# Down-projection units in another order, the final root made per token and transposed, and the squares of a norm in one running sum

## The chip, the cores and the metric

The kernel runs on one core of a Trainium2 chip. The metric is the device time of one execution in microseconds (us), as the median of several runs. The engines are named as in the profile: PE (matrix products), DVE (VectorE), ACT (ScalarE), POOL (GpSimd) and SP (which issues DMAs here).

## The reference

Three transformer layers on 256 tokens of width 1024, in float32. Layer A is a pooling layer, layer B a stick-breaking attention layer, and both end in a gated feed-forward part; a final norm follows, and a second block with attention, a recurrence and a gated output. What the change touches, cut to the core:

```python
def rmsnorm(x, g):
    return x * lax.rsqrt(jnp.mean(x * x, axis=-1, keepdims=True) + EPS) * g

def swiglu(h, w_gu, w_down):                      # D_FF = 2816 = 22 tiles of 128
    gate, up = jnp.split(h @ w_gu, 2, axis=-1)
    return (jax.nn.silu(gate) * up) @ w_down

x = x + swiglu(rmsnorm(x, norm_ffn), w_gu, w_down)      # layers A and B
...
y = merged @ w_out                                # second block, its last part
h = h + _rms_norm(y, g_post)
e = p @ w_ple_up
h = h + jax.nn.sigmoid(h @ w_ple_gate) * e
```

## The kernel before

Activations lie transposed in SBUF: channels on the 128 partitions (8 tiles, `X[:, m, :]`), the 256 tokens along the free dimension. Every float32 operand of the large products is split in an upper part (a copy rounded to fp32r on ACT: `hi`, `XH`, `HH`) and a lower part (the difference, on DVE: `lo`, `XL`, `HL`), and a product is three matmuls, upper by upper, upper by lower and lower by upper (`product`, lines 573 to 575), or two where upper and lower part of the activations stand beside each other (`wide_product`, lines 579 and 580: 256 and 512 columns).

Weights come in units of 1 MB (or 704 KB for a down unit) through four slots. SP loads unit u as soon as PE has finished unit u - 4 (`unit_done`); ACT and DVE split a unit two units ahead of PE, in halves. The order of the work on every engine is a list written out by hand (`plan`), which each engine runs through with its own handlers; engines meet by counting semaphores.

**The feed-forward part.** `gu` computes 22 units, one for each tile of H: PE, then ACT and DVE take the sum, scale it by the norm's root, apply silu, and write `HH` and `HL` (lines 1598 to 1615 and 2259 to 2275). `evac_done` counts the units taken out of PSUM. `down` then computes 8 tiles of the residual from 16 units of 11 tiles each: unit 2m is the first half (h = 0, tiles 0 to 10 of H) of tile m, and unit 2m + 1 the second (h = 1, tiles 11 to 21). The units of even and odd tiles go to two banks of PSUM (`DOWN[turn]`). PE waits for 11 tiles of H ahead of the first unit, and for all 22 ahead of each unit with h = 1. All 16 units run in a loop of four steps. After the second half of a tile DVE adds the two halves of the bank to X (lines 2309 and 2311), ACT writes XH and DVE XL, and POOL squares the tile.

**The norms.** There are eight (n = 0 to 7). POOL squares the 8 tiles and adds them up in two running sums, the even tiles in `ACC[:, 0, :]` and the odd ones in `ACC[:, 1, :]` (`squares`, from line 2916). PE multiplies both by a matrix of ones (lines 664 and 665), so that every partition holds the sum for every token in `STAT`; these are float32 matmuls, which run as two passes each. Where a column per token is wanted as well (n = 3), four more products with one column follow (line 674). DVE scales (line 2089) and takes the reciprocal (2090), ACT the square root (1521).

**The last norm** (n = 7) is that of `y`, between the output projection (`unit_out2`) and the gate (`unit_egate`). DVE copies each pair of tiles of y out of PSUM to `SGT[:, 8:16, :]` (line 2813), ACT squares that copy (1990), and POOL adds up six of the eight squares; PE takes the last two itself (line 669). DVE makes a reciprocal of 256 columns, ACT its root, and `post` on DVE multiplies each tile of y by weight and root and adds it to X (2833, 2835), ACT and DVE split it (1517, 2081), and PE begins the gate with tile 0 (`pair_of`). Between them PE has four short up projections `eup(0)` to `eup(3)` (12 matmuls each, taken out by ACT at line 2001), and eight filler matmuls with ones (`keep_busy`, line 975), which wait for the reciprocal. ACT and DVE split the weights of the second gate unit in that stretch (lines 1773 and 2492), DVE the second half between tiles 0 and 1 of `post`.

```python
second += [("eup", 0), ("stats", 7, 0), ("eup", 1), ("root",), ("eup", 2), ("eup", 3), ("post",)]
```

## Time and profile before

| | us |
|---|---|
| median of 3 runs | 891.33 |
| lowest and highest | 889.78, 893.73 |
| the profiled execution | 892.28 |
| its span, first to last instruction | 890.2 |
| PE busy in it | 872.7 |
| DVE busy | 671.9 |
| ACT busy | 483.4 |
| POOL busy | 115.3 |

Busy time of PE counts each matmul with its whole latency, and these overlap, so that the busy time lies closer to the span than the work of PE does. A start in a timeline is therefore read against the next start. The profiled execution is one execution, 0.95 us above the median.

### The profile page before, as it was taken

How to read it: one execution, taken by the hardware profiler on the slowest of the kernel's cores; microseconds unless marked ns; L12 is line 12 of the kernel's file. 1: busy time of each engine (PE TensorE's matmuls, PEld its weight loads, DVE VectorE, ACT ScalarE, POOL GpSimd, SP SyncE). 2: the span in 40 equal slices, each digit the busy share in tenths (PEclk: the TensorE clock that was granted, in tenths of full speed). 3: DMA queues.
4: the chain of work that ended last, by engine and by line, in shares of the span. 5: the costliest groups of instructions: out<-in, count | busy, mean ns of one | idle time of the engine just before them, and what ended most of it. 6: DMA issues, size and time to landing. Idle time of an engine off the chain costs nothing. (4 is left out here: it accounts for less than half of the span.)

```text
span 890.2 us, 19346 instructions
## 1 busy us (share of the span) xinstructions
PE 872.7 (98%) x7632; PEld 793.1 (89%) x7632; DVE 671.9 (75%) x999; ACT 483.4 (54%) x779; POOL 115.3 (13%) x133
## 2 busy tenths in 40 slices
PE   7999999999999999999999999999999999999998
PEld 7998888888889988898888888899999888899998
DVE  6996887777677776868777767786996777747785
ACT  5674465555545566745555554458624554534453
POOL 2002300000022000050000006640008010000000
PEclk8999999999999999999999999999999999999999
DMA  9443455554557432254555445674534343244441
GB/s 339 176 162 121 154 184 188 186 186 144 171 190 250 149 136 98 93 190 160 182 183 184 175 151 184 203 261 159 180 131 132 122 130 79 95 141 143 167 166 48
DMA packets 23409, 144.48 MB, mean 162 GB/s; under 512 B 2968, under 2 KB 3224, under 8 KB 9648
## 3 DMA queue, kind: packets, MB, share of 16 engines
q1 hardware_dynamic: 22032, 140.26, 45.5%
q0 software_dynamic: 1168, 3.23, 1.6%
q8 instruction: 49, 0.80, 0.4%
q14 instruction: 16, 0.13, 0.0%
q10 hardware_dynamic: 144, 0.06, 0.0%
HBM read 142.47 MB, written 1.06 MB: 161 GB/s over the span
## 5 line engine op out<-in xcount | busy, mean ns | idle before, releaser
L2067 DVE TENSOR_TENSOR lo<-raw,hi 128x1024 fp32r<-128x1024 f32 (+1 forms) x210 | 243.9, 1203 | 12.2 <-ACT hi L1483 8.6
L580 PE MATMUL ps<-X,hi 128*128 128x512 f32 x704 | 249.0, 398 | 0.0
L579 PE MATMUL ps<-X,lo 128*128 128x256 f32 x704 | 198.4, 282 | 0.6 <-DVE X L2082 0.6
L573 PE MATMUL ps<-X,hi 128*128 128x256 f32 x600 | 174.1, 290 | 0.8 <-DVE X L2081 0.7
L574 PE MATMUL ps<-X,hi 128*128 128x256 f32 x600 | 169.7, 283 | 0.0
L575 PE MATMUL ps<-X,lo 128*128 128x256 f32 x600 | 169.6, 283 | 0.0
L580 PEld LDWEIGHTS ps<-X,hi 128*128 128x128 f32 x704 | 132.3, 188 | 32.7
L579 PEld LDWEIGHTS ps<-X,lo 128*128 128x128 f32 x704 | 133.0, 189 | 1.8 <-issue 1.2
L580 PE MATMUL ps<-H,hi 128*128 128x512 f32 x352 | 122.4, 392 | 0.0
L1483 ACT ACTIVATE hi<-raw 128x1024 fp32r<-128x1024 f32 (+1 forms) x109 | 107.7, 988 | 25.0 <-DMA raw<-in_down 13.6
L573 PEld LDWEIGHTS ps<-X,hi 128*128 128x128 f32 x600 | 114.8, 191 | 5.4 <-issue 3.9
L574 PEld LDWEIGHTS ps<-X,hi 128*128 128x128 f32 x600 | 115.0, 192 | 0.4 <-issue 0.2
L575 PEld LDWEIGHTS ps<-X,lo 128*128 128x128 f32 x600 | 114.9, 192 | 0.0
L2492 DVE TENSOR_TENSOR lo<-raw,hi 128x1024 fp32r<-128x1024 f32 x68 | 84.0, 1236 | 30.3 <-ACT hi L1773 23.7
L1486 ACT ACTIVATE hi<-raw 128x1024 fp32r<-128x1024 f32 (+1 forms) x109 | 103.7, 951 | 0.2 <-DMA raw<-in_wide 0.2
L579 PE MATMUL ps<-H,lo 128*128 128x256 f32 x352 | 98.7, 280 | 2.6 <-DVE H L2275 2.6
L580 PEld LDWEIGHTS ps<-H,hi 128*128 128x128 f32 x352 | 65.8, 187 | 14.5
L579 PEld LDWEIGHTS ps<-H,lo 128*128 128x128 f32 x352 | 66.5, 189 | 3.2 <-issue 3.2
L573 PE MATMUL ps<-H,hi 128*128 128x256 f32 x224 | 65.9, 294 | 2.9 <-DVE H L2082 2.6
L574 PE MATMUL ps<-H,hi 128*128 128x256 f32 x224 | 64.5, 288 | 0.0
L575 PE MATMUL ps<-H,lo 128*128 128x256 f32 x224 | 64.5, 288 | 0.0
L1615 ACT ACTIVATE H<-GU 128x256 f32 (+1 forms) x44 | 18.4, 418 | 82.4 <-DVE GU L2268 82.4
(394 smaller groups left out, 1448.7 us busy)
## 6 DMA issues: line engine op xcount, KB each, us to landing
raw<-in_wide SPq DMA_DIRECT2D x106, 1024.0 KB, 4.9
raw<-in_down SPq DMA_DIRECT2D x32, 704.0 KB, 4.1
BI<-bias_table POOLq DMA_DIRECT2D x16, 128.0 KB, 4.8
raw<-in_wide SPq DMA_DIRECT2D x3, 512.0 KB, 9.0
X<-in_x SPq DMA_DIRECT2D x1, 1024.0 KB, 13.0
WG<-in_group SPq DMA_DIRECT2D x1, 768.0 KB, 17.1
out<-X SPq DMA_DIRECT2D x3, 256.0 KB, 2.4
cmask<-in_masks POOLq DMA_DIRECT2D x1, 544.0 KB, 5.9
```

Source lines behind the costliest of these rows:

```text
L573: nc.tensor.matmul(dst, wh, xh, start=first, stop=False, skip_group_check=True)
L574: nc.tensor.matmul(dst, wh, xl, start=False, stop=False, skip_group_check=True)
L575: return nc.tensor.matmul(dst, wl, xh, start=False, stop=last, skip_group_check=True)
L579: nc.tensor.matmul(bank[:, 0:T], wl, x[:, 0, :], start=first, stop=False, skip_group_check=True)
L580: return nc.tensor.matmul(bank, wh, x, start=False, stop=last, skip_group_check=True)
L1483: nc.scalar.activation(hi[:, s, 0:h], raw[:, s, 0:h], ACT.Copy).then_inc(hi_ready, 1)
L1486: nc.scalar.activation(hi[:, s, h:n], raw[:, s, h:n], ACT.Copy).then_inc(hi_ready, 1)
L1615: nc.scalar.activation(dst, src, ACT.Copy).then_inc(hh_ready, 1)
L2067: nc.vector.tensor_tensor(lo[:, s, a:b], raw[:, s, a:b], hi[:, s, a:b].bitcast(F32), ALU.subtract).then_inc(lo_ready, 1)
L2492: nc.vector.tensor_tensor(lo[:, u % 4, part], raw[:, u % 4, part], hi[:, u % 4, part].bitcast(F32), ALU.subtract).then_inc(lo_ready, 1)
```

## The change

The diff has three parts. (1) `down` computes its first four units in the order tile 0 first half, tile 1 first half, tile 0 second half, tile 1 second half, unrolled ahead of the loop, which has a pass less; the weights in HBM lie in that order. (2) The squares of a norm go in one running sum, and PE multiplies that one by ones. (3) The last norm's sum is one column per token; scaling, reciprocal and root are made on that column ([128 x 2]), and PE transposes the root, broadcast along the free dimension, to `STAT`, where `post` reads it. ACT squares the last pair of y from PSUM, DVE copies it after that, the weight splits of the second gate unit stand elsewhere in the lists of ACT and DVE, and the filler matmuls are left out.

```diff
+DN_FIRST = [(0, 0), (1, 0), (0, 1), (1, 1)]
+DN_REST = [(m, h) for m in range(2, KD) for h in range(2)]
...
 # PE, stats(n)
-                pe.wait_ge(sq_done, 8 * (n - 1) if n < 6 else 8 * (n - 2) - 2)
-                nc.tensor.matmul(STAT[:, 0:T], ones[:, :], ACC[:, 0, :], start=True, stop=False, skip_group_check=True)
-                last = nc.tensor.matmul(STAT[:, 0:T], ones[:, :], ACC[:, 1, :], start=False, stop=True, skip_group_check=True)
                 if n == 7:
-                    pe.wait_ge(y_sq, 4)
-                    for m in (6, 7):
-                        last = nc.tensor.matmul(STAT[:, 0:T], ones[:, :], SGT[:, m, :], start=False, stop=(m == 7),
-                                                skip_group_check=True)
+                    pe.wait_ge(sq_done, 8 * (n - 2) - 2)
+                    for q, tile in enumerate((ACC[:, 0, :], SGT[:, 6, :], SGT[:, 7, :])):
+                        if q == 1:
+                            pe.wait_ge(y_sq, 4)
+                        for i in range(2):
+                            last = nc.tensor.matmul(STAT[:, T + i:T + i + 1], tile[:, i * P:(i + 1) * P], ones[:, 0:1],
+                                                    start=(q == 0 and i == 0), stop=(q == 2), skip_group_check=True)
+                    last.then_inc(stat_done, 1)
+                    return
+                pe.wait_ge(sq_done, 8 * (n - 1))
+                last = nc.tensor.matmul(STAT[:, 0:T], ones[:, :], ACC[:, 0, :], start=True, stop=True, skip_group_check=True)
                 if cols:
                     for i in range(2):
-                        for b in range(2):
-                            last = nc.tensor.matmul(STAT[:, T + i:T + i + 1], ACC[:, b, i * P:(i + 1) * P], ones[:, 0:1],
-                                                    start=False, stop=(b == 1), skip_group_check=True)
+                        last = nc.tensor.matmul(STAT[:, T + i:T + i + 1], ACC[:, 0, i * P:(i + 1) * P], ones[:, 0:1],
+                                                start=False, stop=True, skip_group_check=True)
...
 # PE, down(u0): half(u, s, turn, h)
                     if h == 0:
+                        if half_i[0] is None:
+                            bank_free(g0 + turn)
                         else:
+                            pe.wait_ge(evac_done, half_i[0] * 2 + (g0 + turn + 1))
                     if h == 1:
                         pe.wait_ge(hl_ready, N_GU * (layer + 1))
...
-                with pe.Fori(0, N_DN // 4) as i:
+                for j, (m, h) in enumerate(DN_FIRST):
+                    half(u0 + j, (u0 + j) % 4, m, h)
+                with pe.Fori(0, N_DN // 4 - 1) as i:
                     half_i[0] = i
                     for j in range(4):
-                        half(i * 4 + (u0 + j), (u0 + j) % 4)
+                        half(i * 4 + (u0 + 4 + j), (u0 + j) % 4, j // 2, j % 2)
...
 # PE
+            def root():
+                pe.wait_ge(rs_done, 8)
+                for i in range(2):
+                    last = nc.tensor.transpose(STAT[:, i * P:(i + 1) * P], RSC[:, 1, i:i + 1].to_broadcast([P, P]), ident[:, :])
+                last.then_inc(root_in, 1)
...
                 if u == U_EGATE:
-                    pe.wait_ge(rv_done, 8)
-                    keep_busy(8)
...
 # ACT, down: the same four units ahead of its loop; unit_out2(u)
+                if j == 2:
+                    ahead(u + 1)
                 act.wait_ge(xl_ready, 48)
+                if j < 3:
+                    act.wait_ge(evac_done, first_group(u) + 1)
+                    src = SGT[:, 8 + 2 * j:10 + 2 * j, :]
+                else:
+                    act.wait_ge(unit_done, u + 1)
+                    src = PROJ[first_group(u) % 2][:, :].rearrange("p (a b) -> p a b", a=2)
+                nc.scalar.activation(SGT[:, 2 * j:2 * j + 2, :], src, ACT.Square).then_inc(y_sq, 1)
+                if j == 1:
                     ahead(u + 1)
+                if j == 3:
+                    split_half(U_EGATE + 1, 0)
...
 # ACT, eup(j)
-                if j < 2:
-                    split_half(U_EGATE + 1, j)
+                if j == 0:
+                    split_half(U_EGATE + 1, 1)
+
+            def root_column():                       # at ("stats", 7, 0)
+                act.wait_ge(rv_done, 8)
+                nc.scalar.activation(RSC[:, 1, :], RV[:, T:T + 2], ACT.Sqrt).then_inc(rs_done, 1)
...
 # DVE, down: the same four units ahead of its loop; unit_out2(u)
                 dve.wait_ge(unit_done, u + 1)
+                if j == 3:
+                    dve.wait_ge(y_sq, 4)
                 nc.vector.tensor_copy(SGT[:, 8 + 2 * j:10 + 2 * j, :], halves(bank_of(u))).then_inc(evac_done, 1)
...
+                if j == 3:
+                    split_half(U_EGATE + 1, 0)
+
+            def root_column():                       # at ("stats", 7, 0)
+                dve.wait_ge(stat_done, 8)
+                need(dve, rs_done, 7)
+                link(nc.vector.tensor_scalar(RV[:, T:T + 2], STAT[:, T:T + 2], 1.0 / D, EPS, ALU.mult, ALU.add))
+                nc.vector.reciprocal(RV[:, T:T + 2], RV[:, T:T + 2]).then_inc(rv_done, 1)
+                split_half(U_EGATE + 1, 1)
...
 # DVE, post()
-                dve.wait_ge(rs_done, 8)
+                dve.wait_ge(root_in, 1)
...
-                    link(nc.vector.scalar_tensor_tensor(SGT[:, 8 + m, :], SGT[:, 8 + m, :], vec[:, c:c + 1], RS[:, 1, :],
+                    link(nc.vector.scalar_tensor_tensor(SGT[:, 8 + m, :], SGT[:, 8 + m, :], vec[:, c:c + 1], STAT[:, 0:T],
...
-                    if m == 0:
-                        split_half(U_EGATE + 1, 1)
-                    else:
+                    if m > 0:
                         lower_of(m - 1)
...
 # POOL, squares(n, m, src)
-                if m < 2:
-                    nc.gpsimd.tensor_tensor(ACC[:, h, :], src, src, ALU.mult).then_inc(sq_done, 1)
+                if m == 0:
+                    nc.gpsimd.tensor_tensor(ACC[:, 0, :], src, src, ALU.mult).then_inc(sq_done, 1)
                 else:
                     link(nc.gpsimd.tensor_tensor(SQT[:, h, :], src, src, ALU.mult))
                     pool.wait_ge(sq_done, 8 * n + m)
-                    nc.gpsimd.tensor_tensor(ACC[:, h, :], ACC[:, h, :], SQT[:, h, :], ALU.add).then_inc(sq_done, 1)
+                    nc.gpsimd.tensor_tensor(ACC[:, 0, :], ACC[:, 0, :], SQT[:, h, :], ALU.add).then_inc(sq_done, 1)
```

## Rows read from the trace of the kernel before

**Rows 1.** The page: busy time of each engine; granted clock in 40 slices.

```profile
PE 872.7 (98%) x7632; PEld 793.1 (89%) x7632; DVE 671.9 (75%) x999; ACT 483.4 (54%) x779; POOL 115.3 (13%) x133
...
PEclk8999999999999999999999999999999999999999
```

**Rows 2.** Waits of PE: line, releaser, us in total, times, longest us.

```profile
PE ps L579 <- DVE H L2275: 2.6, 2, 1.3
```

**Rows 3.** Timeline of PE, both down projections: start us, us, what [idle].

```profile
225.04 0.28 PE L579 MATMUL ps<-H,lo 128*128 128x256 f32 x1
...
225.39 0.28 PE L579 MATMUL ps<-H,lo 128*128 128x256 f32 x1
...
227.20 0.36 PE L579 MATMUL ps<-H,lo 128*128 128x256 f32 x1 [1.30 <-DVE H L2275]
...
527.06 0.36 PE L579 MATMUL ps<-H,lo 128*128 128x256 f32 x1 [1.30 <-DVE H L2275]
```

**Rows 4.** Timeline of DVE, last gate-up unit of the first layer.

```profile
222.69 0.69 DVE L2259 TENSOR_TENSOR GU<-GU,ps 128x512 f32<-128x512 f32 x1 [1.39 <-ACT GU L1598]
...
226.52 0.43 DVE L2275 TENSOR_TENSOR H<-GU,H 128x256 fp32r<-128x256 f32 x1 [0.48 <-ACT H L1615]
```

**Rows 5.** Timeline of PE, sums of the third and fourth norm.

```profile
102.28 0.59 PE L664 MATMUL ps<-ACC,ones 128*128 128x256 f32 x2
102.71 0.59 PE L665 MATMUL ps<-ACC,ones 128*128 128x256 f32 x2
...
291.09 0.95 PE L674 MATMUL ps<-ones,ACC 128*128 128x1 f32 x8
```

**Rows 6.** Timeline of PE, sum of the last norm to the first gate unit.

```profile
853.86 0.59 PE L664 MATMUL ps<-ACC,ones 128*128 128x256 f32 x2
...
855.78 0.47 PE L573 MATMUL ps<-PH,hi 128*128 128x256 f32 x1
...
860.21 1.95 PE L975 MATMUL ps<-ones 128*128 128x128 f32 x16
862.89 0.36 PE L573 MATMUL ps<-X,hi 128*128 128x256 f32 x1 [0.73 <-DVE X L2081]
```

**Rows 7.** Timeline of DVE, same stretch.

```profile
856.17 0.42 DVE L2089 TENSOR_SCALAR RV<-ps 128x256 f32<-128x256 f32 x1 [1.89 <-PE ps L669]
856.63 1.75 DVE L2090 RECIPROCAL RV<-RV 128x256 f32<-128x256 f32 x1
...
859.47 0.48 DVE L2833 SCALAR_TENSOR_TENSOR SGT<-SGT,vec,RS 128x256 f32<-128x256 f32 x1
...
860.33 1.22 DVE L2492 TENSOR_TENSOR lo<-raw,hi 128x1024 fp32r<-128x1024 f32 x1
...
862.32 0.42 DVE L2081 TENSOR_TENSOR X<-X 128x256 fp32r<-128x256 f32 x1
```

**Rows 8.** Timeline of ACT, same stretch.

```profile
854.32 0.63 ACT L1990 ACTIVATE SGT<-SGT 128x512 f32<-128x512 f32 x1 [2.66 <-DVE SGT L2813]
...
858.08 1.05 ACT L1773 ACTIVATE hi<-raw 128x1024 fp32r<-128x1024 f32 x1
...
859.34 0.59 ACT L2001 ACTIVATE E<-ps 128x512 f32<-128x512 f32 x1
```

**Rows 9.** Single lines (ns min/median/max), and four transposes in the timeline.

```profile
L2309 DVE TENSOR_TENSOR X<-X,ps x16: 420/422/422, 231.4 to 584.5; 128x256 f32 x12, 128x256 f32<-128x256 f32 x4
...
L2642 DVE TENSOR_SCALAR NM<-MX x8: 169/170/171, 692.7 to 754.3; 128x2 f32<-128x2 f32 x8
...
L1523 ACT ACTIVATE RSC<-RV x3: 187/187/188, 24.3 to 595.0; 128x2 f32<-128x2 f32 x3
...
700.47 0.60 PE L1141 MATMUL ps<-ident,PR 128*128 128x128 f32 x4
```

**Rows 10.** Windows, PE: stretch, us, busy (matmuls), clock, DMA share, GB/s.

```profile
9.00:15.00 6.00, 5.02 (x23) 0.52 1.02 398
16.00:20.00 4.00, 4.00 (x36) 1.00 1.01 424
```

More of the change, by code:

```diff
@@ L1630, in half @@
                         split_hi(u + AHEAD, (s + AHEAD) % 4, n)
-                    if (s - u0) % 2 == 1:
+                    if m is not None:
                         act.wait_ge(x_done, m + (8 + 16 * layer + 1))
@@ L2300, in tile, with half @@
                     return a[:, bass.ds(m, 1)] if a is gains else a[:, bass.ds(m, 1), :]
-                def half(u, s, n, m):
-                    odd = (s - u0) % 2 == 1
-                    turn = ((s - u0) % 4) // 2
-                    count = m + (8 + 16 * layer + 1)
+                def half(u, s, n, m, turn):
+                    odd = m is not None
                     if odd:
+                        count = m + (8 + 16 * layer + 1)
                         dve.wait_ge(unit_done, u + 1)
@@ L2322, in half @@
                         split_lo(u + AHEAD, (s + AHEAD) % 4, n)
-                with dve.Fori(0, N_DN // 4 - 1) as i:
+                for j, (m, h) in enumerate(DN_FIRST):
+                    half(u0 + j, (u0 + j) % 4, DN_TILES * P, m if h else None, m)
+                with dve.Fori(0, N_DN // 4 - 2) as i:
                     for j in range(4):
-                        half(i * 4 + (u0 + j), (u0 + j) % 4, DN_TILES * P, i * 2 + j // 2)
+                        half(i * 4 + (u0 + 4 + j), (u0 + j) % 4, DN_TILES * P, i * 2 + (2 + j // 2) if j % 2 else None, j // 2)
                 for j in range(N_DN - 4, N_DN):
                     u = u0 + j
-                    half(u, u % 4, width(u + AHEAD) if u + AHEAD < N_UNITS else 0, j // 2)
+                    half(u, u % 4, width(u + AHEAD) if u + AHEAD < N_UNITS else 0, j // 2 if j % 2 else None, (j % 4) // 2)
             def unit_k(u):
@@ L3038, in down_units @@
 def down_units(w):
-    t = tiles(w).transpose(1, 0, 2, 3)
-    return t.reshape(N_DN, DN_TILES, P, P).transpose(0, 2, 1, 3).reshape(-1, P, DN_TILES * P)
+    t = tiles(w).transpose(1, 0, 2, 3).reshape(KD, 2, DN_TILES, P, P)
+    t = np.stack([t[m, h] for m, h in DN_FIRST + DN_REST])
+    return t.transpose(0, 2, 1, 3).reshape(-1, P, DN_TILES * P)
 def columns(v):
```

33 lines of the change are left out of this document (13 added, 20 removed).

## The prediction

> **What bounds the kernel now.** The page comes first: PE is busy for 872.7 of 890.2 us and its granted clock is full in all slices but the first [rows 1]. So work of PE in the middle of the kernel costs its own time, and what the other engines do costs only where PE waits for them. The next view is PE's list of waits. Its largest entry that the change touches is two waits of 1.3 us, together 2.6 us, for H [rows 2]. The timeline of PE around them is third: they stand at the start of the two down projections. In the dense stretch one 256-column matmul of line 579 follows another after 0.35 us (225.04 to 225.39), but the next starts at 227.20, which is 1.81 us later, so PE loses 1.46 us there, and the same idle time of 1.30 us stands at 527.06 [rows 3]. The page says busy for a matmul's whole latency, so the idle time is shorter than the loss. Last come the timelines of PE, DVE and ACT from 853.86 us, where the last norm's root is made: PE fills part of the wait with eight filler matmuls (1.95 us) and is then idle for 0.73 us more before the gate's first matmul at 862.89 [rows 6].
>
> The profiled execution took 892.28 us, 2.1 us more than its span. The median of the three runs is 891.33, so 0.95 us are taken off when the sum goes over to the median.
>
> **Down units in another order.** The work is the same: as many matmuls, copies, splits and loads, of the same sizes. What moves is the second unit. Before, unit 2 of each layer is the upper half of tile 0, which needs all 22 tiles of H; the last of them is ready at 226.95 (526.9 in the second layer), when line 2275 ends [rows 4]. After, unit 2 is the lower half of tile 1, which needs the first 11 tiles only. PE reaches it at about 225.75. It does wait for one thing more, the evacuation of the last gate-up unit, because the bank check asks for the count of that unit; line 2259 did that at 222.69 and is done at 223.38 [rows 4], 2.4 us early. A down unit takes 11 times 0.35 = 3.9 us [rows 3], so the first unit that needs all of H comes at 225.75 + 3.9 = 229.6, 2.7 us after it is ready. The stall goes, and nothing is late next: 1.46 us for each layer, **2.9 us** in all. Tiles 0 and 1 are now finished one unit apart instead of two, so DVE has two sets of residual additions and lower splits in consecutive units, and POOL two tiles of squares. DVE's additions and lower split go in a unit's 3.9 us at 75% mean load [rows 1] and it had two units without additions before that, so I count nothing. If this cover is not there, the unit after waits and the ends of this term are 0 and 2.9 us.
>
> **One running sum of squares.** Four norms (the third, fourth, fifth and the last) add up their squares in one tile instead of two. In three of them PE drops one product with the matrix of ones. It goes as two passes, and the pair takes 102.71 - 102.28 = 0.43 us [rows 5], with PE dense before and after it, so 3 x 0.43 = 1.3 us. The fourth norm also has eight passes of one column, 0.95 us [rows 5], and half of them go: 0.45 us. Together **1.7 us**. POOL gets one addition more for each norm, at tile 1; it is busy for 13% of the span [rows 1] and the sum is asked for a unit later, so that is hidden. Without that cover the added addition (1 to 1.5 us of POOL) would be PE's wait in three places and this term would be -2.5 us at worst; since the last tile's work on POOL is unchanged, I see no way to it.
>
> **The final root.** The old chain, by the timelines: the sum's products run from 853.86 to 855.78 and include a wait for the square of the last two tiles; DVE starts at 856.17 with 256 columns, and its reciprocal takes 1.75 us; a half weight split lies before the first tile of the residual (859.47) and another of 1.22 us between that tile and the next (860.33), so that the first lower tile starts at 862.32 and PE at 862.89 [rows 6, 7].
>
> The new chain, step by step. ScalarE squares the last tiles straight from PSUM, so it no longer waits for the copy on DVE, and the square (0.63 us [rows 8]) is done before PE asks for it at 853.86. PE then has twelve passes of one column; eight took 0.95 us [rows 5], so 1.4 us, to 855.3 instead of 855.78. Three units of the small up projection took 860.21 - 855.78 = 4.43 us, 1.48 each [rows 6]: the first of them ends at 856.75. In its shadow DVE scales and inverts a [128 x 2] column: the scaling costs 0.17 us [rows 9] and I take as much for the reciprocal of two columns, where 256 took 1.75. With the 0.39 us from the products' end to DVE's start (855.78 to 856.17) and 0.1 us of signals that is 856.1; the root on ACT takes 0.19 us [rows 9], 856.4. PE therefore finds it ready, makes two transposes (four took 0.60 us [rows 9], so 0.3) and is at 857.05, and after two more units at **860.0**. That is PE's own side.
>
> The other side: DVE sees the transposed root at 857.45; the first tile takes 0.86 us (859.47 to 860.33 [rows 7]) and is there at 858.3. ACT is late next: by its order it copies the third up unit, done at about 858.7, first, 0.59 us [rows 8], and splits the residual's tile after it, 0.42 us, so at 859.75; DVE's lower part takes 0.42 and PE 0.15 more [rows 6, 7], which is **860.3**. The later of the two sides is this one, so the gate starts 2.6 us before 862.89. After that DVE gives a tile every 1.2 us, while a tile feeds twelve matmuls, 1.4 us, so the 2.6 us stay. The half weight splits that left the chain (1.05 us each on ACT [rows 8], 1.22 on DVE) move into the time from 853.3 to 857.5, where ACT and DVE had waits of 2.66 and 1.89 us [rows 7, 8]; in this case they cost nothing. The eight filler matmuls fall away inside the wait.
>
> The trace shows neither a one-column pass with this tile and a late partner nor a transpose of a broadcast column. Bounds: passes of 0.10 us and a packed PE give 859.7, a gain of 3.2; passes at the price of those with 256 columns (0.22 us) and transposes at twice theirs give 861.6, a gain of 1.3. I take 2.6, which is nearest to the one-column rows.
>
> DVE now reads the root from PSUM in eight operations. The residual additions from SBUF and from PSUM show no difference in this trace: line 2309 with its source in PSUM takes 0.42 us [rows 9], the lower part of the same size with all of it in SBUF 0.42 [rows 7]. So nothing is in the sum. The Trainium skill (VectorE: DVE Perf Modes, the section on the TRN2 errata) gives VectorE a larger fixed cost with a source in PSUM than in SBUF, 120 against 58 cycles; by it the first of them would come 0.06 us later and the gain would be 2.5 instead of 2.6.
>
> **The sum.** 2.9 + 1.7 + 2.6 = 7.2 us. The profiled execution goes from 892.28 to 885.1, and the median from 891.33 to **884.1**.
>
> **Rivals.**
> - Half of the down term comes back. With two tiles finished in a row, the weights' lower parts of the fourth to sixth unit are late and PE waits there instead. For it: DVE did not have two such units in a row before; against it: 2.7 us of slack at the first one. The gain would be 7.2 - 2.9 = 4.3, so 887.0.
> - The root's chain is longer than PE's cover, because ACT or DVE are still in a weight split when the column root is due. For it: both have two half splits there, 2.1 and 2.4 us of work. Each split that lies in front costs about 1.1 us: gain 1.3, total 5.9, so 885.4.
> - The chip's clock falls, and the kernel gets slower. Place: between 855 and 863 us. The fillers are gone, and in their place are one-column passes, transposes and a short idle time. At the kernel's start the trace has the granted clock at 0.52 over 9 to 15 us, after waits of about 1 us between few matmuls: 23 matmuls are 5.02 us busy there, against 36 in 4.00 us from 16 to 20 us [rows 10], so 0.22 against 0.11 us each. The gate has 192 matmuls; at 1.2 GHz throughout they would cost 192 x 0.107 = 20.5 us more, and the result is 884.1 + 20.5 = 904.6. It would end slower than before from about 67 slow matmuls on, a third of the gate. Against it: the idle times of 1.30 us in the down projections left the clock full [rows 1, 3], and here I expect 0.3 us. The Trainium skill (TensorE: Matmul & The Clock Gate, What's actually happening) calls the throttled state the default that activity releases; by it, leaving out fillers next to a wait can only work against the clock.
> - The change gives nothing measurable, since something else, like the arrival of weights, sets the pace: PE's list of waits shows no wait for a DMA beside the start, so this has little for it. Within 0.5% of before: 887 to 891.
>
> **Chances.** Forecast 0.74, down term lost 0.07, longer root chain 0.12, clock 0.03, nothing 0.04. A difference of about 0.5% (4.5 us) is what a measurement of this kernel can tell, so faster by more means below 886.9. The forecast and the longer chain lie nearly all below it, the lost down term half: faster 0.85, same 0.12, slower 0.03. The range holds the bounds of the unknown costs (gain 6.0 to 7.8) with the scatter of a median of runs that lay 1.5 us below and 2.4 us above theirs: 882.0 to 886.8.
>
> **What would show it.** In PE's waits the entry for H of 2.6 us is gone, and the two norms at 102 and 402 us have two passes instead of four. In the down projections the second unit follows the first with 0.35 us from matmul to matmul, and there is no new wait in units 3 to 6. At the end the first gate matmul comes about 7.2 us earlier than 862.89, at 855.7, some 0.3 us after the last up unit and released by DVE's lower tile, itself released by ACT. The clock is full over that stretch. I would be wrong if the down stall reappears two units later, if PE waits for the root before the transposes, or if the granted clock is below 1.00 in the gate.

## The result, and the profile after

The changed kernel takes 880.93 us (median of 5 runs, 879.88 to 882.52) against 891.50 us for the kernel before (5 runs, 889.78 to 895.03). The ratio is 0.9893, with a 95% interval of 0.9869 to 0.9918: a gain of 10.6 us between the medians (9.5 us by the ratio), where 7.2 us were forecast. The time lies below the forecast's range, which ended at 882.0. The profiled execution took 881.41 us, its span 879.4.

The page of the changed kernel first: busy time by engine and PE's granted clock in 40 slices. Beside [rows 1], PE is busy for 8.9 us less, and the clock is full in the first slice too.

```profile
PE 863.8 (98%) x7612; PEld 787.8 (90%) x7612; DVE 670.4 (76%) x999; ACT 482.9 (55%) x779; POOL 119.5 (14%) x136
...
PEclk9999999999999999999999999999999999999999
```

The down projection of the first layer in PE's timeline (start us, us, engine, line, operation). The second unit starts at 221.59, 0.35 us after the matmul before it, and the third, the first one that needs all of H, at 225.40 in the same way. The idle times of [rows 3] are gone.

```profile
217.77 0.28 PE L582 MATMUL ps<-H,lo 128*128 128x256 f32 x1
...
221.24 0.28 PE L582 MATMUL ps<-H,lo 128*128 128x256 f32 x1
...
221.59 0.28 PE L582 MATMUL ps<-H,lo 128*128 128x256 f32 x1
...
225.40 0.28 PE L582 MATMUL ps<-H,lo 128*128 128x256 f32 x1
```

In DVE's timeline the last tile of H comes 2.5 us before it is asked for, and after that DVE waits 2.94 us before the next residual addition. That answers to [rows 4].

```profile
222.44 0.43 DVE L2299 TENSOR_TENSOR H<-GU,H 128x256 fp32r<-128x256 f32 x1 [0.48 <-ACT H L1624]
...
229.41 0.42 DVE L2332 TENSOR_TENSOR X<-X,ps 128x256 f32<-128x256 f32 x1 [2.94 <-PE ps L583]
```

The sums of the third and the fourth norm in PE's timeline: one product of 256 columns where [rows 5] have two, and then four passes of one column where there were eight.

```profile
100.56 0.59 PE L677 MATMUL ps<-ACC,ones 128*128 128x256 f32 x2
...
284.53 0.59 PE L677 MATMUL ps<-ACC,ones 128*128 128x256 f32 x2
284.96 0.50 PE L680 MATMUL ps<-ones,ACC 128*128 128x1 f32 x4
```

The end, in PE's timeline. PE waits 0.62 us for POOL's sum at 844.34, the twelve passes of one column follow, and then matmuls of the up projection take 0.41 us where the same line took 0.28 at 842.14. The gate begins at 852.05, where [rows 6] have 862.89.

```profile
842.14 0.28 PE L576 MATMUL ps<-PH,hi 128*128 128x256 f32 x1
...
844.34 0.58 PE L672 MATMUL ps<-ones,ACC 128*128 128x1 f32 x4 [0.62 <-POOL ACC L3031]
844.78 1.03 PE L672 MATMUL ps<-ones,SGT 128*128 128x1 f32 x8
...
846.17 0.41 PE L576 MATMUL ps<-PH,hi 128*128 128x256 f32 x1
...
848.09 0.63 PE L1419 MATMUL ps<-ident,RSC 128*128 128x128 f32 x2
...
852.05 0.35 PE L576 MATMUL ps<-X,hi 128*128 128x256 f32 x1
```

PE by windows (stretch, us, busy and count of PE, PEld, DVE, ACT, POOL, then PE's granted clock, DMA share, GB/s). The clock stood at 0.50, the 1.2 GHz level, over 3.4 us.

```profile
844.30:846.00 1.70, 1.66 (x15) 1.69 (x16) 1.24 (x2) 1.70 (x3) 0.00 (x0) 1.00 0.96 405
846.00:849.40 3.40, 3.40 (x19) 3.40 (x18) 2.00 (x5) 0.96 (x3) 0.00 (x0) 0.50 0.15 58
```

The two profiles compare as follows, by the starts of the same matmuls. "Passes" stands for the products with the matrix of ones, of which each one runs as two passes: a norm has four passes of 256 columns before and two after.

| stretch | before, us | after, us | difference |
|---|---|---|---|
| kernel's start to the first gate-up matmul of layer A | 95.91 | 94.14 | -1.77 |
| that to the first pass of the third norm's sum | 6.37 | 6.42 | +0.05 |
| third norm's passes | 0.68 | 0.24 | -0.44 |
| rest of gate-up, layer A | 118.90 | 116.97 | -1.93 |
| down, layer A | 62.40 | 60.78 | -1.61 |
| fourth norm's passes | | | -0.88 |
| fifth norm's passes | 0.68 | 0.24 | -0.44 |
| rest of gate-up, layer B | 118.90 | 117.03 | -1.87 |
| down, layer B | 62.40 | 60.78 | -1.61 |
| first up projection to first gate matmul | 10.45 | 9.91 | -0.54 |
| all else | | | +0.20 |
| span | 890.23 | 879.39 | -10.84 |

Three rows had no place in the forecast: the start of the kernel, which the change doesn't touch, and the two gate-up loops, which lost 1.9 us each behind the passes. The final root brought 0.54 us where 2.6 were forecast.

The loops are shorter because PE's matmuls come a little faster. The timeline of the kernel before, in the middle of the first gate-up loop: four pairs of lines 579 and 580 take 151.19 - 149.78 = 1.41 us.

```profile
149.78 0.28 PE L579 MATMUL ps<-X,lo 128*128 128x256 f32 x1
...
151.19 0.28 PE L579 MATMUL ps<-X,lo 128*128 128x256 f32 x1
```

The changed kernel at the same place (the lines are now 582 and 583): 151.21 - 149.83 = 1.38 us for four pairs.

```profile
149.83 0.28 PE L582 MATMUL ps<-X,lo 128*128 128x256 f32 x1
...
151.21 0.28 PE L582 MATMUL ps<-X,lo 128*128 128x256 f32 x1
```

Over the whole loop the mean is 353.3 ns a pair before and 346.7 ns after. The granted clock is full in either. In the slow rhythm two pairs in three take longer (in turn 346, 355 to 356 and 358 to 359 ns), where in the fast one all lie at 344 to 350 ns; no idle time and no releaser stands beside it. A gate-up layer has 352 pairs and a down layer 176, so the slow rhythm costs 2.2 us in a gate-up loop (118.90 against 116.67 below) and 1.2 us in a down loop. The Trainium skill (TensorE: Matmul & The Clock Gate, Back-to-back issue gap) gives N / 2.4 + 2.5 ns for the gap of an isolated warm matmul, and says that a stream with a weight load ahead of each goes otherwise; by the formula 109 and 216 ns here, 325 ns for the pair as an estimate. The trace has 346.7 or 353.3, so neither rhythm is at that figure.

### The profile page after: what moved, and what is told of

The parts are those of the page before. It is cut to its first block and busy times, and to the rows that moved or that the text cites. A ratio compares the mean times of both kernels' runs of the same rounds, so it can differ in the third digit from the quotient of the medians.

```text
span 879.4 us, 19235 instructions
## 1 busy us (share of the span) xinstructions
PE 863.8 (98%) x7612; PEld 787.8 (90%) x7612; DVE 670.4 (76%) x999; ACT 482.9 (55%) x779; POOL 119.5 (14%) x136
## 5 line engine op out<-in xcount | busy, mean ns | idle before, releaser
L583 PE MATMUL ps<-X,hi 128*128 128x512 f32 x704 | 244.7, 392 | 0.0
L582 PE MATMUL ps<-H,lo 128*128 128x256 f32 x352 | 98.1, 279 | 0.0
L576 PE MATMUL ps<-H,hi 128*128 128x256 f32 x224 | 65.0, 290 | 3.3 <-DVE H L2106 2.9
L577 PE MATMUL ps<-H,hi 128*128 128x256 f32 x224 | 63.3, 283 | 0.0
L578 PE MATMUL ps<-H,lo 128*128 128x256 f32 x224 | 63.3, 283 | 0.0
```

Source lines behind the costliest of these rows:

```text
L576: nc.tensor.matmul(dst, wh, xh, start=first, stop=False, skip_group_check=True)
L577: nc.tensor.matmul(dst, wh, xl, start=False, stop=False, skip_group_check=True)
L578: return nc.tensor.matmul(dst, wl, xh, start=False, stop=last, skip_group_check=True)
L582: nc.tensor.matmul(bank[:, 0:T], wl, x[:, 0, :], start=first, stop=False, skip_group_check=True)
L583: return nc.tensor.matmul(bank, wh, x, start=False, stop=last, skip_group_check=True)
```

## The experiments

Ratios are to the kernel before on the same chip, with a 95% interval; the sets ran on several chips, and the kernel before had medians of 888.75 to 891.61 us on them. Pace and tail are read from one profiled execution of each run. "Pair" is the mean time from one matmul of line 579 (582) to the next in a gate-up loop.

**Each part of the change alone, and the whole again.** Only the order of the down units (`a_only`), only the running sum (`b_only`), only the final root (`c_only`; with two running sums it has sixteen passes of one column), and the changed kernel once more (`after_again`).

```diff
 a_only: kernel before, with
+                for j, (m, h) in enumerate(DN_FIRST):
+                    half(u0 + j, (u0 + j) % 4, m, h)
 b_only: kernel before, with
-                nc.tensor.matmul(STAT[:, 0:T], ones[:, :], ACC[:, 0, :], start=True, stop=False, ...)
-                last = nc.tensor.matmul(STAT[:, 0:T], ones[:, :], ACC[:, 1, :], start=False, stop=True, ...)
+                last = nc.tensor.matmul(STAT[:, 0:T], ones[:, :], ACC[:, 0, :], start=True, stop=(n != 7), ...)
 c_only: kernel before, with the new stats(7), root_column, root, post and orders of the last stage, and
+                    for q, tile in enumerate((ACC[:, 0, :], ACC[:, 1, :], SGT[:, 6, :], SGT[:, 7, :])):
```

> The kernel before with the new order of the down units alone. Theory: both stalls of 1.46 us at the second down unit go and nothing comes in their place, 2.9 to 3.2 us less (0.9967 to 0.9964 of before). The gate-up stage keeps its slow rhythm, 0.353 us for a pair of matmuls of lines 579 and 580 (118 us for 21 units), since four float32 passes of the norm's sum still stand ahead of it. Rival: the faster gate-up rhythm (0.347 us a pair, 117 us) comes with the new down order or by chance of the execution; then it shows here and the kernel gains 6.7 us.

> The kernel before with one running sum of squares alone (all four norms; the last norm's sum still over 256 columns). Theory: 0.43 + 0.88 + 0.43 + 0.43 us of passes go, and with two passes instead of four ahead of the gate-up loop its pairs come every 0.347 us instead of 0.353, 1.9 us less in each layer: 6.0 us in all, 0.9933 of before. The down stalls of 1.46 us stay. Rival: the rhythm has nothing to do with the passes; then 2.2 us, 0.9976.

> The kernel before with the final root per token alone; its sum still has two running sums, so 16 one-column passes. Theory of the prediction: 2.2 to 2.6 us less. What the trace of the changed kernel suggests instead: 0.5 us less if the granted clock falls again where the one-column passes and the transposes stand (12 matmuls at 0.21 us instead of 0.12) and if the square of the third pair of y waits again behind a weight split whose load is late. Rival: both were chance of one execution; then 2 us or more.

> The changed kernel once more, unchanged. What is bound to the program repeats: gate-up pairs at 0.347 us, no down stall, 0.43 us less for the sum of two norms. What was chance of one execution does not: the granted clock over 5 to 20 us (1.00 in the first trace, 0.50 to 0.92 before), the loads of 7 to 8 us in the output projection, and the fall of the clock between 846 and 849 us.

| kernel | median, us | before, us | ratio | gate-up A, B (us) | pair (ns) | down A, B (us) | tail (us) |
|---|---|---|---|---|---|---|---|
| a_only | 891.08 | 891.61 | 0.9992 [0.9976, 1.0007] | 118.91, 118.91 | 353.3 | 61.95, 61.95 | 10.06 |
| b_only | 888.20 | 891.61 | 0.9971 [0.9949, 0.9993] | 117.03, 117.04 | 346.7 | 62.40, 62.39 | 10.08 |
| c_only | 889.96 | 891.61 | 0.9968 [0.9952, 0.9984] | 118.91, 118.80 | 353.3, 353.0 | 62.40, 62.45 | 7.96 |
| after_again | 881.33 | 891.61 | 0.9891 [0.9859, 0.9923] | 117.04, 117.06 | 346.7 | 60.78, 60.78 | 7.72 |

Gate-up is counted from behind the passes; the tail goes from the first up projection to the gate. Single parts bring 0.8, 2.9 and 3.2 thousandths, 6.9 together, and the whole 10.9. The root does what it should in `c_only` and `after_again`. The order of the down units removes the stall in `a_only` and still brings 0.45 us a layer only, because the down loop now runs in the slow rhythm from end to end. Where the stall is left in (`before`, `c_only`), the matmuls behind it come in the fast rhythm: the stall was paid back in part. It looked as if two passes ahead of the loop (`b_only`) gave the fast rhythm and four the slow one. But `b_only` gained 3.4 us between the medians where 6.0 were expected with that rhythm, and its ten executions went from 886.09 to 894.63 us, so the profiled one (886.81) need not stand for the rest.

**Is it the number of passes?** The changed kernel with its product issued twice (four passes), and the kernel before with a third one (six passes); the first product is overwritten by the next.

```diff
 after_four: changed kernel
                 pe.wait_ge(sq_done, 8 * (n - 1))
+                if n in (2, 4):
+                    nc.tensor.matmul(STAT[:, 0:T], ones[:, :], ACC[:, 0, :], start=True, stop=True, ...)
 before_six: kernel before, the same lines
```

> The changed kernel with the sum's product over ones done twice ahead of both gate-up loops (the first result is overwritten), so four float32 passes stand there again as before the change. Theory (the passes ahead set the rhythm): each layer pays 0.43 us for the passes, 1.86 us for the gate-up stage at 0.353 us a pair, and 1.15 us because the down stage, which has no stall any more, goes on in the slow rhythm: 3.4 us a layer, 6.9 us in all, about 888 us. Rival (the rhythm hangs on something else that the change brought, as the single sum on POOL): 0.9 us, about 882 us.

> The kernel before with a third product over ones ahead of both gate-up loops, so six passes. One look for the rhythm: if the number of passes acts through what is left over after a fixed beat, six may give 0.347 us a pair (gate-up stage 1.9 us shorter in each layer); if more passes always mean the slow rhythm, it stays 0.353 us. The passes themselves cost 0.43 us in each layer.

`after_four` had a slow loop A (118.91, down 61.95) and a fast loop B (116.67, 60.78) in one and the same execution; ratio 0.9946 [0.9931, 0.9962]. `before_six` was fast in both gate-up loops (116.68, 116.67; one run, 887.77 us), and its down loop A was slow with 352.9 ns although it has the stall. So four passes don't make the slow rhythm by themselves. The tail of `after_four` lost to the clock as that of the first profile: PE waited 1.15 us for POOL, and the next up projections ran at 1.2 GHz. PE's timeline, and the window behind it:

```profile
848.18 0.58 PE L672 MATMUL ps<-ones,ACC 128*128 128x1 f32 x4 [1.15 <-POOL ACC L3033]
848.62 1.20 PE L672 MATMUL ps<-ones,SGT 128*128 128x1 f32 x8
```

```profile
850.04:852.17 2.13, 2.13 (x11) 2.13 (x11) 1.54 (x4) 0.52 (x2) 0.00 (x0) 0.50 0.03 8
```

**Does an interruption of PE reset the rhythm?** `a_only`, in which PE also waits for DVE's reciprocal behind the sum.

```diff
                 stats(2 + 2 * layer, False)
+                pe.wait_ge(rv_done, 3 + 2 * layer)
```

> The new down order alone, and PE waits after the norm's sum, with its four passes, until DVE's reciprocal is done: a stall of about 2.6 us ahead of the gate-up loop. Theory (a stall of PE ends the slow rhythm, whatever the passes before it were): pairs at 0.347 us through gate-up and down, so 1.9 + 1.15 us come back in each layer against 2.6 us of stall: 0.4 to 0.9 us less than the down order alone, and a stall that costs less than nothing. Rival (only the passes decide): pairs stay at 0.353 us and the kernel is 5.2 us slower than the down order alone.

All four loops had pairs of 346.7 ns and down took 60.78 us, as the theory has it. That the stall did it isn't shown: the clock fell in the same place, and there are only two layers, in one execution. It cost far more than it gave: 898.97 us, ratio 1.0128 [1.0105, 1.0151]. The wait was 3.85 us and not the 2.6 us expected, DVE being in a weight split when the sum was done; the first six pairs behind it took 510 to 644 ns in layer A and the first nine 640 to 780 ns in B, at the lower clock. PE's timeline and a window:

```profile
102.41 0.59 PE L667 MATMUL ps<-ACC,ones 128*128 128x256 f32 x2
106.86 0.36 PE L581 MATMUL ps<-X,lo 128*128 128x256 f32 x1 [3.85 <-DVE RV L2093]
```

```profile
107.40:109.90 2.50, 2.50 (x9) 2.15 (x8) 1.70 (x3) 1.76 (x3) 0.00 (x0) 0.50 0.03 7
```

**The tail.** `tail_best` puts ACT's third square ahead of a weight split and the first tile of `XH` ahead of the third copy; `after_x0` does the second alone.

```diff
 both
-                    if m == 0:
-                        eup(3)
+                    if m == 0:
+                        eup(2)
+                        eup(3)
 tail_best only: ACT's ahead(u + 1) one step later
-                if j == 2:
-                    ahead(u + 1)
...
-                if j == 1:
+                if j in (1, 2):
                     ahead(u + 1)
```

> The changed kernel with two orders on ACT changed: the square of the third pair of y ahead of the weight split that waits for its load, and the first upper tile of the residual ahead of the copy of the third up unit. Theory: PE has no wait for POOL's sum (0.13 and 0.78 us in the two traces of the changed kernel) and none for the first lower tile (about 0.35 us): 0.4 to 0.5 us less where the clock stays full, 0.9995 of the changed kernel, not to be seen in the times but in the trace. Rival: ACT's copy of the third up unit is then late for the bank of the gate, and PE waits there instead.

> The changed kernel with one order on ACT changed: in the last norm it makes the first upper tile of the residual ahead of its copy of the third up unit. Theory (the first lower tile waits for that copy, as predicted): the gate starts 0.3 to 0.4 us earlier after the root, at most 7.4 us after the first up matmul where the changed kernel had 7.7 with a full clock. In the times 0.04%, not to be told from the changed kernel. Rival: the copy is then late for the bank that the gate needs, and nothing is won.

`tail_best`: 882.52 us, ratio 0.9932 [0.9913, 0.9952], tail 8.06 us. The later split came back as a wait of 0.31 us for DVE. `after_x0`: 884.45 us, ratio 0.9921 [0.9903, 0.9939]; its tail is the shortest, 7.21 us, and 0.26 us of that return behind the gate's start (27.60 us to the end, 27.3 elsewhere). Neither ratio is below those of the changed kernel (0.9893 and 0.9891 so far). `after_x0` had a slow loop A (119.11 us) with two passes: the first case against the rule "two passes, fast".

**One kernel, several executions.** `after_four_2` and `after_four_3` are `after_four` again, and `passes_ab` and `passes_ba` put one and two dummy products of one column (two passes each) ahead of the sums of layer A and B, or the other way round.

```diff
 passes_ab (1, 2), passes_ba (2, 1): kernel before
+                for _ in range((1, 2)[layer]):
+                    nc.tensor.matmul(STAT[:, T:T + 1], ones[:, :], ones[:, 0:1], start=True, stop=True, ...)
                 stats(2 + 2 * layer, False)
```

> The changed kernel with four passes ahead of the gate-up loops, once more. In the first look layer A was slow (353.3 ns a pair) and layer B fast (346.7). If the rhythm belongs to the program, the same again: gate-up 118.9 us in A and 116.7 in B. If it belongs to the single execution, another pattern.

> The kernel before with dummy products of one column (two passes of 0.11 us each) ahead of the sum's four passes: one in layer A, two in layer B. A look at what decides the rhythm. If the delay or count ahead of the loop acts as a phase, A and B differ from each other, and from the 353.3 ns a pair of the kernel before in at least one layer. If four passes of 256 columns always lead to the slow rhythm, both stay at 353.3 and the gate-up stages at 118.9 us.

> The same with two dummy products in layer A and one in layer B. If the count decides, the layers swap their rhythms against the run before; if something of the layer decides, they keep them.

`after_four_2` was fast in A (116.67) and slow in B (118.80), the reverse of `after_four`, at 884.56 us. `passes_ab`: both fast (116.67, 116.68; 887.61 us). `passes_ba`: A slow (118.91), B fast (116.67; 891.70 us). The program alone doesn't fix the rhythm: it differs between executions of one program, layer by layer. Whether the number of passes changes the odds was then the question, asked with the unchanged kernel before twice, `b_only` again and `after_four` a third time; the edits are nothing or as above.

> The kernel before, unchanged, in another execution. If its four one-column passes make the slow rhythm likely: both gate-up loops at about 118.9 us (353.3 ns a pair). If the rhythm is drawn afresh at even odds whatever stands ahead: a fast layer (about 116.7 us) in one of two.

> The kernel before once more, for the same count: slow in both layers if the passes load the odds, mixed if they don't.

> The kernel before with the one running sum alone (two passes). If two passes load the odds for the fast rhythm: both gate-up loops at about 117.0 us. If the rhythm is drawn at even odds: slow (118.9) in one of two.

> The changed kernel with its sum's product issued twice (four passes). So far one layer of two was slow in each of two executions. If the count of passes sets the odds: at least one layer slow (118.8 to 118.9 us). If it is what the rest of the changed kernel does that makes the fast rhythm: both fast.

| execution | us | gate-up A | gate-up B | down A | down B |
|---|---|---|---|---|---|
| before_2 | 886.09 | 116.67 fast | 116.67 fast | 62.40 | 62.40 |
| before_3 | 890.64 | 118.90 slow | 116.67 fast | 62.40 | 62.40 |
| b_only_2 | 892.50 | 119.11 slow | 119.15 slow | 63.49 | 63.52 |
| after_four_3 | 887.75 | 118.91 slow | 118.80 slow | 61.95 | 61.96 |

The kernel before can be fast in both layers. That execution took 886.09 us, 5.2 us under the first median and 3.2 us under another execution on the same chip (889.28); its span is 6.2 us shorter than that of the first profile, 4.4 us of it in the gate-up loops and 1.6 us at the kernel's start. Two passes can be slow in both layers. Here are the loop's first matmul and the down projection's first matmul in `before_2`, for the 116.67:

```profile
101.36 0.47 PE L579 MATMUL ps<-X,lo 128*128 128x256 f32 x1
...
218.03 0.28 PE L579 MATMUL ps<-H,lo 128*128 128x256 f32 x1
```

**Where the rhythm turns.** In the traces of all twenty executions the pace of a layer changes in three places alone: behind the norm's passes, at the third gate-up unit, and at the stall in the down projection. Behind two passes all sixteen layers were fast, and the four that ended slow turned at the third unit. Behind four passes eight of sixteen were slow at once, and three more turned at the third unit. With four passes the pace ahead of them went with the outcome too: of ten layers that came to them fast all ended slow, of six that came slow five ended fast. This was counted after the runs and holds for four passes with nothing added (`before_six` and `passes_ab` have layers that came fast and stayed fast). PE's timeline of `after_third`, layer B: twelve pairs take 402.81 - 398.65 = 4.16 us ahead of the third unit and 408.45 - 404.20 = 4.25 us in it.

```profile
398.65 0.28 PE L582 MATMUL ps<-X,lo 128*128 128x256 f32 x1
...
402.81 0.28 PE L582 MATMUL ps<-X,lo 128*128 128x256 f32 x1
...
404.20 0.28 PE L582 MATMUL ps<-X,lo 128*128 128x256 f32 x1
...
408.45 0.28 PE L582 MATMUL ps<-X,lo 128*128 128x256 f32 x1
```

**The wait that was hidden in the loops.** Where the rhythm is the same, the stretch from the sum's first pass to the down projection hardly shrinks: 117.35 us in `before_2`, 117.27 in `b_only`, 117.28 in `after_again`. The product saved is 0.44 us, so most of it comes back. PE's timeline of the changed kernel at the third gate-up unit has 0.45 us between two starts that are 0.23 apart elsewhere:

```profile
106.31 0.39 PE L583 MATMUL ps<-X,hi 128*128 128x512 f32 x1
106.76 0.35 PE L582 MATMUL ps<-X,lo 128*128 128x256 f32 x1
```

DVE's timeline: the addition that frees the first unit's bank of PSUM ends at 106.51, and it stands behind reciprocal, root and, before these, a weight split to 102.66, which doesn't come earlier when the sum does.

```profile
97.08 5.58 DVE L2091 TENSOR_TENSOR lo<-raw,hi 128x1024 fp32r<-128x1024 f32 x4
102.58 0.41 DVE L2113 TENSOR_SCALAR RV<-ps 128x256 f32<-128x256 f32 x1
...
105.82 0.69 DVE L2283 TENSOR_TENSOR GU<-GU,ps 128x512 f32<-128x512 f32 x1 [1.04 <-ACT GU L1607]
```

`root_split` lets DVE make the root between the halves of that split; `after_third` is the changed kernel beside it.

```diff
-                split_lo(u0 + AHEAD, (u0 + AHEAD) % 4, UNIT)
+                split_lo(u0 + AHEAD, (u0 + AHEAD) % 4, UNIT, (0,))
                 rstd(2 + 2 * layer, False)
+                split_lo(u0 + AHEAD, (u0 + AHEAD) % 4, UNIT, (1,))
```

> The changed kernel, with DVE making the third and fifth norm's root between the two halves of a weight split instead of behind both. If the wait of PE ahead of the third gate-up unit (a pair of 647 and 694 ns where others have 347) is for DVE's addition of the first unit, which stands behind that split, the addition starts about 1 us earlier, the pair is back at 347 and the stretch from the sum's first pass to the first down matmul goes from 117.2 to 116.9 us with the fast rhythm (119.35 to 119.1 with the slow one), in both layers; in the time that is 0.6 us. If the wait is for something else (weights, or the queue of PE after the passes), the pair stays at 640 to 730.

> The changed kernel, unchanged, on the same chip, for the comparison and as one more execution for the count of rhythms and of falls of the clock in the tail. If two passes load the odds: both layers fast, 117.0 us. If the odds are even: one of two slow. Tail 7.7 us with a full clock, about 10 if it falls; the time 0.6 us above that of the kernel with the split root if the scatter lets it be seen.

The wait is gone in both layers: the stretch is 116.92 us (100.90 to 217.82 and 395.58 to 512.50), as expected, and neither layer turned slow at the third unit. DVE's and PE's timelines of `root_split`:

```profile
97.47 4.45 DVE L2091 TENSOR_TENSOR lo<-raw,hi 128x1024 fp32r<-128x1024 f32 x3
101.84 0.41 DVE L2113 TENSOR_SCALAR RV<-ps 128x256 f32<-128x256 f32 x1
...
103.96 1.17 DVE L2091 TENSOR_TENSOR lo<-raw,hi 128x1024 fp32r<-128x1024 f32 x1
105.09 0.69 DVE L2283 TENSOR_TENSOR GU<-GU,ps 128x512 f32<-128x512 f32 x1
```

```profile
100.90 0.38 PE L677 MATMUL ps<-ACC,ones 128*128 128x256 f32 x1
...
106.31 0.39 PE L583 MATMUL ps<-X,hi 128*128 128x512 f32 x1
106.54 0.28 PE L582 MATMUL ps<-X,lo 128*128 128x256 f32 x1
...
217.82 0.28 PE L582 MATMUL ps<-H,lo 128*128 128x256 f32 x1
```

`root_split` takes 880.19 us (879.00 to 881.50), ratio 0.9899 [0.9878, 0.9920]; `after_third` 883.43 us (880.23 to 884.31), ratio 0.9925 [0.9902, 0.9948], both against 888.75. The wait explains 0.7 of the 3.2 us between the two medians. Loop B of `after_third` was slow in its profile (119.15, down 61.96) and `root_split` was fast in both, and the intervals overlap. Its median is the lowest of all, but its ratio isn't below the first two of the changed kernel (0.9893, 0.9891), so that it is the better kernel is shown by the trace alone.

## Why the prediction was wrong

In the two profiles, the step that failed and put the time below the forecast is one that had no term: that PE's dense stream goes at one pace, "0.35 us" from one 256-column matmul to the next, before and after the change. The runs showed two paces, 346.7 and 353.3 ns a pair, in executions of one and the same kernel, and this makes 4.5 us between the two profiles. Of the terms that were there, the running sum was too large (1.7 us forecast, about 1.0 measured) and the down units somewhat too small (2.9 forecast, 3.2 measured). How much of the medians' 10.6 us is pace stays open, since only the profiled executions show it.

**Down units (2.9 us forecast).** The mechanism was right: no stall, and nothing late in units 3 to 6; H had 2.5 us of slack, forecast 2.7. The two profiles give 1.61 us a layer where I had 1.46. The price depends on the rhythm, which I did not have: where all is fast, 62.40 goes to 60.78 (1.62 us); where the loop is slow, the stall brought the fast rhythm back in five of eight cases, and what is left of the gain against those is 62.40 to 61.95 (0.45 us, `a_only`). For both layers that is 3.2 or 0.9 us; my ends were 2.9 and 0, so the upper one was too low, since it took the stall for all that there was.

**One running sum (1.7 us forecast).** The passes brought just that: 0.44, 0.88 and 0.44. The step that failed in this term is "with PE dense before and after it": that PE is dense says that a matmul costs its time, not that what PE waits for next comes sooner too. In the third and the fifth norm PE reaches the third gate-up unit before DVE has freed the bank, and 0.30 to 0.39 us of 0.44 return. `root_split` showed it. I had looked at POOL as cover and not at the bank. Net it is some 1.0 us.

**The final root (2.6 us forecast).** Right with a full clock: 10.45 to 7.72 in `after_again`, 2.7 us. With a full clock the new tail takes 7.51 to 8.02 us in six executions, and the old one 10.06 to 10.45 in ten. The order of events was the one forecast. PE's timeline of `after_again`:

```profile
844.75 0.58 PE L672 MATMUL ps<-ones,ACC 128*128 128x1 f32 x4
...
846.08 0.36 PE L576 MATMUL ps<-PH,hi 128*128 128x256 f32 x1
...
847.58 0.38 PE L1419 MATMUL ps<-ident,RSC 128*128 128x128 f32 x2
...
850.91 0.36 PE L576 MATMUL ps<-X,hi 128*128 128x256 f32 x1
```

ACT's third up copy, and the upper part of tile 0 after it, were late next, as I had put it; ACT's timeline:

```profile
849.41 0.60 ACT L2021 ACTIVATE E<-ps 128x512 f32<-128x512 f32 x1 [1.04 <-PE ps L578]
849.90 0.41 ACT L1526 ACTIVATE X<-X 128x256 fp32r<-128x256 f32 x1
```

The twelve passes took 1.33 us (844.75 to 846.08), forecast 1.4; the first tile came 0.41 us after the transposes began, forecast 0.7 (0.3 for the transposes, which take 0.13 us here, and 0.4 behind them). DVE's operation with the root in PSUM takes 0.48 us, as the one with it in SBUF did [rows 7]: the longer fixed cost that the Trainium skill gives for a source in PSUM (VectorE: DVE Perf Modes, the TRN2 errata) isn't seen.

```profile
846.26 0.16 DVE L2849 TENSOR_SCALAR RV<-ps 128x2 f32<-128x2 f32 x1
...
847.99 0.48 DVE L2869 SCALAR_TENSOR_TENSOR SGT<-SGT,vec,ps 128x256 f32<-128x256 f32 x1 [0.25 <-PE ps L1419]
```

**The clock.** It was a rival with 3 in 100, and in the first profile it came true in small: 12 matmuls at 0.21 us, a tail of 9.91 us, 2.2 more than in `after_again`. Of ten executions with the new tail, two had it, `after` (PE waited 0.62 us for POOL's sum, then twelve one-column passes) and `after_four` (1.15 us). The other eight had waits of 0.31 us or less and a full clock. That the wait brings it was not tested by itself. Its place was right, and its price never came near 20 us, because the clock returned after 3.4 us. What made PE wait was POOL's addition of the third pair's squares, which ACT makes behind a weight split whose load came late (in `after` at 841.09, 1.05 us before the up projection; in `after_again` 1.75 us before). I had checked the square of the last pair only. The Trainium skill (TensorE: Matmul & The Clock Gate, What's actually happening) calls this state the default that activity releases. The trace agrees in so far as the clock fell behind waits of 0.62 and 1.15 us; the idle times of 1.30 us in the down projections left it full [rows 3].

**What had no term: PE's rhythm, 4.5 us in this pair of profiles.** There the span fell by 10.8 us, 3.6 more than the 7.2 forecast: rhythm 4.5 and the start 1.8 on one side, the root's lost 2.1 (the clock) and the 0.7 us that came back in the loops on the other. The kernel before was slow in both gate-up loops in the profile that I read, and the changed one fast in both in its. The matmul starts were before me in [rows 3]; I read 0.35 us and not 0.3533 against 0.3467. Compare executions with the same rhythm, `before_2` and `after_again`, and leave the start out: loops with their passes -0.11, down -3.24, fourth norm's passes -0.88, tail -2.50, together 6.7 us. That is what the change itself does in one pair of executions at equal pace, on two chips, against 7.2 forecast. That the sum comes so near is partly luck: down is 0.3 us above its term, the running sum 0.7 below.

**The start of the kernel, 1.8 us.** The same code ran at a mean clock of 0.77 in one profile and 1.00 in the other. Before, 5 to 20 us, and after:

```profile
5.00:20.00 15.00, 12.44 (x76) 11.84 (x76) 13.00 (x18) 10.48 (x17) 2.38 (x2) 0.77 1.00 389
```

```profile
5.00:20.00 15.00, 12.05 (x89) 11.47 (x89) 13.01 (x19) 10.42 (x17) 2.39 (x2) 1.00 1.02 399
```

`after_third`, the same program as `after`, had 0.77 there. So the change didn't bring it.

**How much of the gain is chance?** That stays open in part. By the ratios of three sets of runs (`after`, `after_again`, `after_third`) the changed kernel gained 1.07, 1.09 and 0.75 per cent, 9.5, 9.7 and 6.7 us, where equal rhythms give 6.7. Of sixteen layers with four passes of 256 columns and nothing else ahead of the loop (eight executions of `before`, `a_only`, `c_only` and `after_four`) eleven were slow; of sixteen with two passes (the changed kernel, `b_only`, the two of the tail, `root_split`) four were. If layers were independent, so uneven a split would be rare with equal odds; but two layers share an execution, and these were counted after the question had come up. So that fewer passes make the fast rhythm likelier is suggested and not shown, and neither is that a kernel without the wait at the third unit (`root_split`, one profile) stays fast. What keeps the beat was not found: a full clock, no semaphore and no idle time stand beside it.

The sign was right. The range was too narrow: it had the scatter of a median but took the rhythm of the one profile as given, and one execution can differ from the next by up to 6.8 us (two layers of 2.2 and 1.2 us) for that alone. Three of its sums don't close, and none of them bears on the miss: with 1.3 us for the root the lower end of the gain is 5.9 and not 6.0 us, 2.4 us above that is 887.8 and not 886.8, and the rival that loses "half" of the down term takes off the whole 2.9 us.

## What to carry to other kernels

Read the pace of a long loop to a tenth of a nanosecond (first and last start, divided by the count), in both kernels and in more than one execution, before a gain of 1% is put down to an edit; compare stretches in executions of the same pace. A product taken out of a dense PE is worth its time only up to the next wait on another engine: look one or two units on, at what frees the bank. A stall that is removed may have been setting a rhythm right, as it did here in five of eight slow layers.

## What the runs showed of the hardware

- A stream of pairs of 256 and 512 columns in fp32r goes at 346.7 or 353.3 ns a pair with a full clock, over hundreds of pairs. In forty layers it changed only behind the norm's passes, at the third gate-up unit or at the down projection's stall, and it differed between executions of one program. The stall ahead of the down projection's second unit came behind a slow gate-up loop eight times: the loop behind it was fast in five (`before` twice, `before_3`, `c_only` twice) and slow in three (`b_only_2` twice, `passes_ba`). Behind a fast one it stayed fast in nine of ten.
- Idle times of 1.30 us between dense matmuls left the clock full [rows 3]; 3.85 us in `a_reset` and 0.62 us with twelve one-column passes behind in `after` were followed by 1.2 GHz. The matmuls at that level took 0.21 us against 0.12.
- A float32 pass of one column takes 0.11 us (twelve from 844.75 to 846.08), and one of 256 columns 0.22 [rows 5]: half the time for 1/256 of the columns.
